# An expert's row capacity cut from 128 to 96 in the mixture stage of a two-layer decoder trunk

## The chip, the cores and the metric

The kernel runs on one core of a Trainium2 chip. The metric is the device time of one execution in microseconds (us); a comparison takes medians over several executions. The instruction streams belong to TensorE (PE; its weight loads are listed apart as PEld), VectorE (DVE), ScalarE (ACT), GpSimd (POOL) and SyncE (SP), which issues most of the DMAs.

## What is computed

Two decoder layers over 256 tokens of width 1024, in float32. Layer 0 is latent attention and retention, then a dense gated feed-forward part; layer 1 is sliding-window and stick-breaking attention, then a mixture of 8 experts of which every token takes 2. The change lies in the mixture:

```python
def _moe(h, router, w_gate, w_up, w_down):
    xf = h.reshape(T, D)
    logits = (xf @ router).astype(jnp.float32)
    top_logits, top_idx = lax.top_k(logits, TOP_K)
    gates = jax.nn.softmax(top_logits, axis=-1)
...
    def expert_block(args):
        xb, e = args
        return (jax.nn.silu(xb @ w_gate[e]) * (xb @ w_up[e])) @ w_down[e]
```

`w_gate` and `w_up` are 1024 x 3584 and `w_down` is 3584 x 1024 for each expert, float32. The 512 choices (256 tokens, two each) are spread over the experts as the router says; the outputs, scaled by the gates, are added to their tokens' rows. The final norm follows.

## The kernel before

**Precision.** Each float32 operand is split in two fp32r parts, a high one (a rounded copy, made by ScalarE) and a low one (the difference, made by VectorE). `mm3` (line 288) multiplies with three matmuls, lines 290, 291 and 292: high by high, high by low, low by high. The first operand is the stationary one, which an instruction of its own loads (LDWEIGHTS in the profile); the second is the moving one.

**The weight stream.** All weights pass through a ring in SBUF: 14 slots of 1 MB in the mixture. SyncE issues a load when VectorE has split the slot's old content. A slot is two units of 128 x 1024; `hi_unit` (line 295) and `lo_unit` (line 301) split a unit into one of four pairs of buffers `w_hi`, `w_lo`, which TensorE gives back when it has multiplied with it.

**One expert** (`moe_pe`, `moe_act`, `moe_dve`, from line 1769 on). The expert's tokens stand in CAP = 128 places. `xe_hi`, `xe_lo` hold their rows turned, 8 blocks of 128 features by CAP places. In the matmuls the token side is stationary and the weights move, 512 columns at a time: `gate_up` gives a bank of [places, 512] for each of 7 chunks of 512 hidden features, ScalarE applies SiLU and VectorE multiplies into `eh`. `turn` (line 1931) transposes `eh` in four matmuls against the identity into bank 6, [features, 4 x CAP]; ScalarE copies it to `hT_hi` and VectorE takes the difference `hT_lo`. `down` multiplies these with `w_down` and accumulates in banks 4 and 5. In such a transpose the data is stationary and the identity moves. The order on TensorE is written by hand, so that each product's inputs were made one chunk earlier.

**Getting and putting rows.** `prepare_pick` compares the places' numbers (`iota`, from 128 x part + 1 on) with the tokens' positions in the expert. `rows_pe` (line 1723) makes token number and gate of each place with four short matmuls. POOL gathers the next expert's rows from DRAM to `xe_rows` (line 1754), and adds the scaled outputs of the expert to the tokens' rows in DRAM, `h_rows` (line 1759); free places go to spare rows behind the 256 real ones. `turn_rows` (line 1706) transposes the gathered rows, eight matmuls. The first expert's rows are gathered by matmul instead (`gather_pe`, line 1699), and the last expert's outputs are put back by matmul with `pickT`.

**The general path.** Every engine runs the eight experts once (`part` 0), then reads the count of the fullest expert and compares it with CAP:

```python
        def overflow(eng, body, most):

            with eng.If(most > CAP):
                body(eng, 1)
```

Where it is larger, all eight experts are run again for the places from 129 to 256.

Of the kernel before, what the change touches and what calls it, by code (L numbers as in the profile page):

```python
# [37 lines left out]
CAP = 128  # L38
# [18 lines left out]
def moe_items():  # L57
# [9 lines left out]
    ident=128, g_ab=8, eps=8, incl=128, negones=128, ones=128, before=128, strict=128, iota=264, cos_m=64, sin_m=64,  # L67
# [10 lines left out]
def trunk(nc, x, consts, decay_t, ab_w_in, w_uq, w_ukv, ab_w_out, f_gate, f_up, f_down,  # L78
          cd_w_in, cd_w_out, router, m_gate, m_up, m_down, moe_gain, final_gain, out):
    with ExitStack() as ctx:  # L80
# [91 lines left out]
        eh = [place(f"eh{i}", [P, FC], at=ARENA + 2048 * i) for i in range(2)]  # L172
# [4 lines left out]
        y_hi = place("y_hi", [P, D], F32R, at=ARENA + 8192)  # L177
        y_rows = place("y_rows", [P, D], at=ARENA + 8192)
        xe_rows = place("xe_rows", [P, D], at=XT_AT + 12288)
        y_lo = place("y_lo", [P, D], F32R, at=XT_AT + 12288)  # L180
        pick = place("pick", [P, TB, CAP], at=ARENA + 12288)
        tok_gate = place("tok_gate", [P, TB, NE + 1], at=ARENA + 13312)
        row_from = place("row_from", [P, 1], U32, at=ARENA + 13440)
        row_next = place("row_next", [P, 1], U32, at=ARENA + 13472)
        row_to = place("row_to", [P, 1], U32, at=ARENA + 13504)
        gate_next = place("gate_next", [P, 1], at=ARENA + 13536)
        place_gate = place("place_gate", [P, 1], at=ARENA + 13568)
        spare_row = place("spare_row", [P, 1], at=ARENA + 13600)
        h_rows = nc.dram_tensor("h_rows", (256 + CAP, D), F32).ap()
        xn_rows = nc.dram_tensor("xn_rows", (256, D), F32).ap()  # L190
        pickT = place("pickT", [P, TB, P], F32R, at=ARENA + 14336)
# [1492 lines left out]
        def gather_act(act, r, q):  # L1684
            act.wait_ge(gather_banked, 2 * q + (r + 1))
            nc.scalar.activation(xe_hi[:, 4 * r:4 * r + 4, :].rearrange("p k t -> p (k t)"), pb[2 + r],
                                 ACT.Copy).then_inc(gather_hi, 1)

        def gather_dve(dve, r, q):
            dve.wait_ge(gather_hi, 2 * q + (r + 1))  # L1690
            nc.vector.tensor_tensor(xe_lo[:, 4 * r:4 * r + 4, :].rearrange("p k t -> p (k t)"), pb[2 + r],  # L1691
                                    f32(xe_hi[:, 4 * r:4 * r + 4, :].rearrange("p k t -> p (k t)")),
                                    ALU.subtract).then_inc(gathered, 1)

        def gather_pe(pe, r):
            for kk in range(4):
                k = 4 * r + kk
                for tb in range(TB):
                    ins = nc.tensor.matmul(pb[2 + r][:, kk * P:kk * P + P], xn[:, tb, k * P:k * P + P],
                                           pick[:, tb, :], start=tb == 0, stop=tb == 1)  # L1700
# [18 lines left out]
        def rows_pe(pe, q):  # L1719

            pe.wait_ge(pick_done, 2 * q + 2)
            for tb in range(TB):
                ins = nc.tensor.matmul(pb[7][:, 0:NE + 1], pick[:, tb, :], tok_gate[:, tb, :], start=tb == 0,
# [3 lines left out]
        def rows_dve(dve, e, q, part):  # L1727

            dve.wait_ge(rows_banked, q + 1)
            found = pb[7][:, 0:1]  # L1730
            nc.vector.tensor_scalar(spare_row, found, 0.0, const("spare"), ALU.is_equal, ALU.mult).then_inc(spare_done, 1)
            nc.vector.tensor_scalar(row_from, found, -1.0, 0.0, ALU.add, ALU.max)
            nc.vector.tensor_copy(gate_next, pb[7][:, one(e + 1)])
# [35 lines left out]
        def moe_act(act, part):  # L1769
            def silu_(c, q):  # L1770
# [3 lines left out]
                nc.scalar.activation(eh[c % 2], pb[2 * (c % 2)], ACT.Silu).then_inc(e_silu, 1)  # L1774

            def turned(c, q):
# [5 lines left out]
                nc.scalar.activation(hT_hi[c % 2].rearrange("p j t -> p (j t)"), pb[6], ACT.Copy).then_inc(hT_done, 1)  # L1782

            def outputs(q, last):
                act.wait_ge(row_ready, q + 1)
                for n in range(2):
# [5 lines left out]
                    nc.scalar.activation(dst[:, n * 512:n * 512 + 512], pb[4 + n], ACT.Copy,  # L1792
# [38 lines left out]
        def moe_dve(dve, part):  # L1831
            def product(c, q):
                dve.wait_ge(*m_used("u", c, q))
                dve.wait_ge(e_silu, 7 * q + (c + 1))
                nc.vector.tensor_tensor(eh[c % 2], eh[c % 2], pb[2 * (c % 2) + 1], ALU.mult).then_inc(e_prod, 1)

            def rest(c, q):
                dve.wait_ge(hT_done, 7 * q + (c + 1))
                nc.vector.tensor_tensor(hT_lo[c % 2].rearrange("p j t -> p (j t)"), pb[6],  # L1839
# [3 lines left out]
            def outputs_rest(q):  # L1843
                for n in range(2):
                    w = slice(n * 512, n * 512 + 512)
                    dve.wait_ge(y_scaled, 2 * q + (n + 3))
                    nc.vector.scalar_tensor_tensor(out=y_lo[:, w], in0=pb[4 + n], scalar=place_gate,
# [10 lines left out]
            def expert(e, q, last):  # L1858
                for c in range(1, NFC):
# [8 lines left out]
                    if c == 1:  # L1868
                        if last:
                            dve.wait_ge(pgt_banked, part + 1)  # L1870
                            nc.vector.tensor_scalar(pickT.rearrange("p b t -> p (b t)"), pb[7][:, 0:256], 0.0, None,
# [42 lines left out]
        def moe_pe(pe, part):  # L1914
            def gate_up(kind, c, q, units=slice(0, 4)):
                bank = pb[2 * (c % 2) + (kind == "u")]
# [9 lines left out]
            def turn(c, q):  # L1926
# [21 lines left out]
            def down_last(q):  # L1948
                pe.wait_ge(hT_lo_done, 7 * q + (LAST + 1))
                units = m_units(("d", LAST))  # L1950
                for t, nn in ((0, 0), (0, 1), (1, 0), (1, 1), (2, 0), (3, 0), (2, 1), (3, 1)):
# [4 lines left out]
                    ins = mm3(pb[4 + nn], hT_hi[LAST % 2][:, t, :], hT_lo[LAST % 2][:, t, :], w_hi[:, buf, w],  # L1956
# [16 lines left out]
            def expert(q, last):  # L1973
                for c in range(1, NFC):
# [3 lines left out]
                    if c == 1 and last:  # L1978
                        pe.wait_ge(rows_done, q + 1)
                        pe.wait_ge(pick_done, 2 * q + 2)  # L1980
                        for tb in range(TB):
                            ins = nc.tensor.transpose(pb[7][:, tb * P:tb * P + P], pick[:, tb, :], const("ident"))
# [161 lines left out]
        def overflow(eng, body, most):  # L2144

            with eng.If(most > CAP):
                body(eng, 1)
# [176 lines left out]
def shape_tables(np):  # L2324
# [11 lines left out]
    t["iota"] = np.broadcast_to(np.arange(264, dtype=f), (P, 264))  # L2336
# [65 lines left out]
```

## Time and profile before

| | |
|---|---|
| median of 3 runs | 1550.05 us (1549.32 to 1550.11) |
| the profiled execution's own time | 1550.45 us |
| its span, first to last instruction | 1548.7 us |
| mean granted TensorE clock | 0.993 |
| TensorE busy | 1514.1 us, 98% of the span |
| weight loads | 1245.4 us, 80% |
| VectorE busy | 1269.4 us, 82% |
| ScalarE busy | 1105.1 us, 71% |
| POOL busy | 25.9 us, 2% |
| bytes read from HBM | 447.33 MB |

How to read it: the profile is one execution. A row of a group of instructions gives the line of the code, the engine, the operation, what it writes and reads, its shapes and its count, then the busy time and the mean duration, and the idle time of the engine in front of it with what ended that. Matmuls overlap: each lasts longer than the distance from its start to the start of the next, and the end is modelled, so the pace of TensorE is read from starts, or from the chain of waits, whose pieces don't overlap. A shape `128*96` of a matmul or a weight load is rows by columns of the stationary operand, and the `128x512` behind it the moving operand or, for a weight load, what is loaded. The granted clock is 1.00 for 2.4 GHz and 0.50 for 1.2 GHz.

### The profile page before, as it was taken

The page shows a single profiled execution, that of the slowest core. Times are in us where ns is not written, and L with a number is a line of the kernel's source. Part 1 is how long each engine was busy: PE and PEld are TensorE (multiplying, and loading weights), DVE is VectorE, ACT ScalarE, POOL GpSimd, SP SyncE. Part 2 cuts the span into 40 slices and gives each one's busy share as a digit, 9 for nine tenths or more (in the row PEclk, how much of TensorE's full clock was granted, in tenths as well). Part 3 has the DMA queues.
Part 4 walks back from the last instruction along what each step waited for, and adds up shares of the span by engine and source line. Part 5 has one row for each costly group of instructions (what it writes and reads, how often), then busy time and mean ns, then how long its engine had stood idle before and what let it go on. Part 6 is the DMA issues. An engine that isn't in the chain of part 4 may idle for free.

```text
span 1548.7 us, 22163 instructions
## 1 busy us (share of the span) xinstructions
PE 1514.1 (98%) x7290; PEld 1245.4 (80%) x7290; DVE 1269.4 (82%) x1553; ACT 1105.1 (71%) x1380; POOL 25.9 (2%) x21
## 2 busy tenths in 40 slices
PE   7999999999999999999999999999999999999997
PEld 6778788888777678888888888888888888888885
DVE  4577576666667668999999999999999999999997
ACT  5565455555466648888888888788788788878885
POOL 0000000000000000000000000000000000000000
PEclk9999999999999989999999999999999999999999
DMA  8433365455544569999999999999999999999970
GB/s 328 168 131 112 129 226 213 163 205 201 190 164 152 187 232 344 377 375 368 389 372 366 387 382 360 387 389 354 389 387 350 394 387 349 399 383 349 403 277 29
DMA packets 193176, 454.88 MB, mean 294 GB/s; under 512 B 8160, under 2 KB 12128, under 8 KB 192864
## 3 DMA queue, kind: packets, MB, share of 16 engines
q1 hardware_dynamic: 190288, 443.69, 77.6%
q0 software_dynamic: 2832, 10.49, 2.7%
q8 instruction: 30, 0.49, 0.1%
q14 instruction: 26, 0.21, 0.0%
HBM read 447.33 MB, written 6.82 MB: 293 GB/s over the span
## 4 chain that ended last, share of the span: by engine, by line
PE 95%; DVE 4%; ACT 1%; issue 0%; DMA 0%; SPq 0%; DVEq 0%; ACTq 0%
PE bank L290 26%; PE bank L292 25%; PE bank L291 25%; PE bank L1431 7%; PE bank L1433 3%; PE bank L1931 2%; DVE w_lo L303 1%; PE bank L360 1%; PE bank L1271 1%; PE bank L788 1%; PE bank L1262 0%; PE bank L777 0%; DVE xT_both L330 0%; PE bank L1706 0%; DMA h<-x_dram 0%
## 5 line engine op out<-in xcount | busy, mean ns | idle before, releaser
L303 DVE TENSOR_TENSOR w_lo<-ring_low,w_hi 128x1024 fp32r<-128x1024 f32 (+2 forms) x442 | 533.5, 1217 | 100.2 <-ACT w_hi L299 76.5
L299 ACT ACTIVATE w_hi<-ring_low 128x1024 fp32r<-128x1024 f32 (+2 forms) x442 | 466.1, 1056 | 134.0 <-PE bank L292 133.6
L303 DVE TENSOR_TENSOR w_lo<-ring,w_hi 128x1024 fp32r<-128x1024 f32 x336 | 404.4, 1222 | 38.0 <-ACT w_hi L299 15.9
L299 ACT ACTIVATE w_hi<-ring 128x1024 fp32r<-128x1024 f32 x336 | 355.1, 1063 | 81.5 <-PE bank L292 81.4
L290 PE MATMUL bank<-w_hi,xe_hi 128*128 128x512 f32 x896 | 353.8, 395 | 0.4 <-DVE xe_lo L1691 0.4
L292 PE MATMUL bank<-w_hi,xe_lo 128*128 128x512 f32 x896 | 349.7, 390 | 0.0
L291 PE MATMUL bank<-w_lo,xe_hi 128*128 128x512 f32 x896 | 348.9, 389 | 0.0
L292 PEld LDWEIGHTS bank<-w_hi,xe_lo 128*128 128x128 f32 x896 | 168.2, 188 | 35.9
L290 PEld LDWEIGHTS bank<-w_hi,xe_hi 128*128 128x128 f32 x896 | 168.3, 188 | 34.2 <-DVE xe_lo L1691 0.6
L291 PEld LDWEIGHTS bank<-w_lo,xe_hi 128*128 128x128 f32 x896 | 168.4, 188 | 34.0
L290 PE MATMUL bank<-w_hi,hT_hi 128*128 128x512 f32 x448 | 177.5, 396 | 0.0
L292 PE MATMUL bank<-w_hi,hT_lo 128*128 128x512 f32 x448 | 176.0, 393 | 0.0
L291 PE MATMUL bank<-w_lo,hT_hi 128*128 128x512 f32 x448 | 175.7, 392 | 0.0
L1431 PE MATMUL bank<-xT_both,w_hi 128*128 128x512 f32 x448 | 159.0, 399 | 0.0
L1433 PE MATMUL bank<-xT_both,w_lo 128*128 128x256 f32 x448 | 126.3, 282 | 0.0
L1431 PEld LDWEIGHTS bank<-xT_both,w_hi 128*128 128x128 f32 x448 | 84.8, 189 | 20.1
L292 PEld LDWEIGHTS bank<-w_hi,hT_lo 128*128 128x128 f32 x448 | 84.2, 188 | 19.0
L291 PEld LDWEIGHTS bank<-w_lo,hT_hi 128*128 128x128 f32 x448 | 84.4, 188 | 18.2
L290 PEld LDWEIGHTS bank<-w_hi,hT_hi 128*128 128x128 f32 x448 | 84.3, 188 | 18.3 <-DVE hT_lo L1839 0.3
L1416 DVE TENSOR_TENSOR w_lo<-ring_low,w_hi 128x1024 fp32r<-128x1024 f32 x56 | 68.5, 1224 | 34.0 <-ACT w_hi L1408 32.5
L290 PE MATMUL bank<-w_hi,xT_both 128*128 128x512 f32 (+3 forms) x224 | 89.2, 398 | 4.7 <-DVE w_lo L303 3.8
L1433 PEld LDWEIGHTS bank<-xT_both,w_lo 128*128 128x128 f32 x448 | 85.3, 191 | 0.3
(301 smaller groups left out, 1621.7 us busy)
## 6 DMA issues: line engine op xcount, KB each, us to landing
ring<-m_gate_dram SPq DMA_DIRECT2D x72, 1024.0 KB, 5.8
ring_low<-m_down_dram SPq DMA_DIRECT2D x72, 1024.0 KB, 6.2
ring<-m_up_dram SPq DMA_DIRECT2D x56, 1024.0 KB, 6.0
ring_low<-m_up_dram SPq DMA_DIRECT2D x56, 1024.0 KB, 6.5
ring_low<-m_gate_dram SPq DMA_DIRECT2D x40, 1024.0 KB, 5.6
ring<-m_down_dram SPq DMA_DIRECT2D x40, 1024.0 KB, 6.8
ring_low<-f_gate_dram SPq DMA_DIRECT2D x14, 1024.0 KB, 5.1
ring_low<-f_up_dram SPq DMA_DIRECT2D x14, 1024.0 KB, 5.4
```

The lines of the kernel that those rows point to most:

```text
L290: nc.tensor.matmul(out_, a_hi, b_hi, start=first, stop=False, **kw)
L291: nc.tensor.matmul(out_, a_hi, b_lo, start=False, stop=False, **kw)
L292: return nc.tensor.matmul(out_, a_lo, b_hi, start=False, stop=last, **kw)
L299: nc.scalar.activation(w_hi[:, buf, 0:width], src, ACT.Copy).then_inc(hi_ready, 1)
L303: nc.vector.tensor_tensor(w_lo[:, buf, 0:width], src, f32(w_hi[:, buf, 0:width]), ALU.subtract).then_inc(split_ready, 1)
L360: ins = nc.tensor.matmul(pb[bank][half_rows(r), cols], v[r][0 if first else 1], a[r][:, src], start=first, stop=not first, skip_group_chec ...
L788: ins = nc.tensor.matmul(pb[((7, 4), (5, 6))[tb][nh]][:, 0:384], latT[:, k, tb * P:tb * P + P], ring[4 + nh][:, k * 384:k * 384 + 384], st ...
L1271: ins = nc.tensor.transpose(pt_bank(i)[:, b * P:b * P + P], p_sb1[i % 2][:, 1 + b * P:1 + b * P + P], const("ident"))
L1416: nc.vector.tensor_tensor(f_split(w_lo, u), f_block(kind, u), f32(f_split(w_hi, u)), ALU.subtract).then_inc(split_ready, 1)
L1431: nc.tensor.matmul(pb[j], w_hi[:, j, w], xT_both[:, :, k, :], start=k == 0, stop=False, skip_group_check=True)
L1433: ins = nc.tensor.matmul(pb[j][:, 0:256], w_lo[:, j, w], xT_hi[:, k, :], start=False, stop=k == KD - 1, skip_group_check=True)
L1931: ins = nc.tensor.transpose(pb[6][:, j * P:j * P + P], eh[c % 2][:, j * P:j * P + P], const("ident"))
```

## The change

CAP becomes 96. Every tile and every bank slice with a place per partition has 96 partitions instead of 128, every one with a place per column has 96 columns. The general path runs the experts again in two further parts, for the places 97 to 192 and 193 to 288, instead of one; the table `iota` becomes longer for that.

```diff
-CAP = 128
+CAP = 96
+PARTS = 3
...
-        eh = [place(f"eh{i}", [P, FC], at=ARENA + 2048 * i) for i in range(2)]
+        eh = [place(f"eh{i}", [CAP, FC], at=ARENA + 2048 * i) for i in range(2)]
...
-        xe_rows = place("xe_rows", [P, D], at=XT_AT + 12288)
+        xe_rows = place("xe_rows", [CAP, D], at=XT_AT + 12288)
...
-                ins = nc.tensor.transpose(pb[2 + r][:, kk * P:kk * P + P], xe_rows[:, k * P:k * P + P],
-                                          const("ident"))
+                ins = nc.tensor.transpose(pb[2 + r][:, kk * CAP:kk * CAP + CAP], xe_rows[:, k * P:k * P + P],
+                                          const("ident")[0:CAP, 0:CAP])
...
-                nc.scalar.activation(hT_hi[c % 2].rearrange("p j t -> p (j t)"), pb[6], ACT.Copy).then_inc(hT_done, 1)
+                nc.scalar.activation(hT_hi[c % 2].rearrange("p j t -> p (j t)"), pb[6][:, 0:4 * CAP], ACT.Copy).then_inc(hT_done, 1)
...
-                bank = pb[2 * (c % 2) + (kind == "u")]
+                bank = pb[2 * (c % 2) + (kind == "u")][0:CAP]
...
-                    ins = nc.tensor.transpose(pb[6][:, j * P:j * P + P], eh[c % 2][:, j * P:j * P + P],
-                                              const("ident"))
+                    ins = nc.tensor.transpose(pb[6][:, j * CAP:j * CAP + CAP], eh[c % 2][:, j * P:j * P + P],
+                                              const("ident")[0:CAP, 0:CAP])
...
-                        ins = mm3(pb[4 + nn], hT_hi[c % 2][:, t, :], hT_lo[c % 2][:, t, :], w_hi[:, buf, w],
+                        ins = mm3(pb[4 + nn][0:CAP], hT_hi[c % 2][:, t, :], hT_lo[c % 2][:, t, :], w_hi[:, buf, w],
...
-                body(eng, 1)
+                for part in range(1, PARTS):
+                    body(eng, part)
```

`xe_hi`, `xe_lo`, `hT_hi`, `hT_lo` and `pick` were written with CAP before and change with it. The engines' lists up to the branch keep their order; shapes change, and what is skipped behind the branch grows. TensorE in the loop over experts, at the transposes of the first chunk, before (here the shape behind a product is the written bank's partitions by the moving columns, behind a transpose the written partitions by columns):

```order
L292 MATMUL bank<-w_hi,xe_lo 128x512
L1927 REGISTER_ALU
L1931 MATMUL bank<-cst,eh_124 128x128 x4
L1918 REGISTER_ALU
L290 MATMUL bank<-w_hi,xe_hi 128x512
L291 MATMUL bank<-w_lo,xe_hi 128x512
```

and now (lines are one higher):

```order
L293 MATMUL bank<-w_hi,xe_lo 96x512
L1928 REGISTER_ALU
L1932 MATMUL bank<-cst,eh_124 128x96 x4
L1919 REGISTER_ALU
L291 MATMUL bank<-w_hi,xe_hi 96x512
L292 MATMUL bank<-w_lo,xe_hi 96x512
```

The products are as many and move as many columns; the transposes write and move 96 columns instead of 128. POOL at the end of part 0 and behind the branch, before:

```order
L1651 TENSOR_LOAD cnt_i
L1651 ISA x2
L1765 DMA h<-h_rows 128x2x1024
L2146 COMPARE_AND_BRANCH
L1745 DMA h_rows<-h 128x2x1024
L1754 DMA xe_rows<-xn_rows,row_from 128x1024
L1759 DMA h_rows<-y_rows,row_to 384x1024
```

and now:

```order
L1652 TENSOR_LOAD cnt_i
L1652 ISA x2
L1766 DMA h<-h_rows 128x2x1024
L2147 COMPARE_AND_BRANCH
L1746 DMA h_rows<-h 128x2x1024
L1755 DMA xe_rows<-xn_rows,row_from 96x1024
L1760 DMA h_rows<-y_rows,row_to 352x1024

```

The indirect transfers have 96 rows instead of 128, and behind the one branch stand two further parts instead of one (the second is not shown).

## Rows read from the trace of the kernel before

**Rows 1.** The page: span, and granted clock in 40 slices of 38.7 us
```profile
span 1548.7 us, 22163 instructions
...
PEclk9999999999999989999999999999999999999999
```

**Rows 2.** Waits, 620 us to the end: who waited for whom, total us, times, longest
```profile
POOL h_rows L1759 <- issue: 419.4, 7, 59.9
...
ACT w_hi L299 <- PE bank L292: 168.2, 564, 0.6
DVE w_lo L303 <- ACT w_hi L299: 19.7, 58, 1.3
...
PE bank L1969 <- DVE y_lo L1847: 0.3, 1, 0.3
```

**Rows 3.** Waits of the SyncE queue, 620 us to the end
```profile
SPq L1636 <- DVE w_lo L303: 696.5, 307, 3.5
```

**Rows 4.** Chain of waits, pieces of three stretches: start us, us, what
```profile
28.71 3.43 PE bank L777 x8
...
46.54 3.87 PE bank L788 x12
...
1052.03 0.87 PE bank L1706 x8
...
1091.76 0.44 PE bank L1931 x4
1092.19 0.35 PE bank L1723 x4
...
1171.63 0.87 PE bank L1706 x8
```

**Rows 5.** Groups of instructions on PE, by form: count, busy us, mean ns, idle before
```profile
L290 PE MATMUL bank<-w_hi,xe_hi 128*128 128x512 f32 x896 | 353.8, 395 | 0.4 <-DVE xe_lo L1691 0.4
...
L290 PE MATMUL bank<-w_hi,hT_hi 128*128 128x512 f32 x448 | 177.5, 396 | 0.0
...
L1931 PE MATMUL bank<-cst,eh 128*128 128x128 f32 x224 | 33.5, 272 | 0.0
...
L1706 PE MATMUL bank<-cst,xe_rows 128*128 128x128 f32 x56 | 7.2, 272 | 0.0
```

**Rows 6.** Timeline of the stage from 900 us: start us, us, engine, line, operation
```profile
900.01 0.39 PE L290 MATMUL bank<-w_hi,xe_hi 128*128 128x512 f32 x1
...
903.18 0.39 PE L292 MATMUL bank<-w_hi,xe_lo 128*128 128x512 f32 x1
```

**Rows 7.** Groups of weight loads (PEld), by form
```profile
L290 PEld LDWEIGHTS bank<-w_hi,xe_hi 128*128 128x128 f32 x896 | 168.3, 188 | 34.2 <-DVE xe_lo L1691 0.6
...
L1931 PEld LDWEIGHTS bank<-cst,eh 128*128 128x128 f32 x224 | 27.7, 140 | 7.3
...
L797 PEld LDWEIGHTS bank<-cst,kcat 128*96 128x96 f32 x16 | 1.8, 125 | 0.3
```

**Rows 8.** Timeline of PE in layer 0, products of 288 columns
```profile
14.24 0.44 PE L291 MATMUL bank<-w_lo,xT_both 128*128 128x288 f32 x1
...
16.64 0.44 PE L292 MATMUL bank<-w_hi,xT_both 128*128 128x288 f32 x1
...
17.47 0.29 PE L290 MATMUL bank<-w_hi,xT_both 128*128 128x288 f32 x1
...
19.33 0.30 PE L292 MATMUL bank<-w_hi,xT_both 128*128 128x288 f32 x1
```

**Rows 9.** Stretches: us, busy (count) by engine, PEclk, DMA share, GB/s
```profile
13.00:17.00 4.00, 3.16 (x13) 3.16 (x14) 2.79 (x5) 3.98 (x8) 0.00 (x0) 0.61 0.96 405
18.00:20.00 2.00, 2.00 (x18) 2.00 (x16) 1.09 (x3) 1.64 (x2) 0.00 (x0) 1.00 1.04 394
...
820.00:920.00 100.00, 100.00 (x452) 82.50 (x451) 92.68 (x91) 81.28 (x84) 3.31 (x2) 1.00 1.03 381
```

**Rows 10.** Groups of instructions on DVE by form, 620 to 1500 us
```profile
L1839 DVE TENSOR_TENSOR hT_lo<-bank,hT_hi 128x512 fp32r<-128x512 f32 x51 | 34.8, 683 | 0.0
```

More of the change, by code:

```diff
@@ L1685, in gather_act @@
             act.wait_ge(gather_banked, 2 * q + (r + 1))
-            nc.scalar.activation(xe_hi[:, 4 * r:4 * r + 4, :].rearrange("p k t -> p (k t)"), pb[2 + r],
+            nc.scalar.activation(xe_hi[:, 4 * r:4 * r + 4, :].rearrange("p k t -> p (k t)"), pb[2 + r][:, 0:4 * CAP],
                                  ACT.Copy).then_inc(gather_hi, 1)
@@ L1690, in gather_dve @@
             dve.wait_ge(gather_hi, 2 * q + (r + 1))
-            nc.vector.tensor_tensor(xe_lo[:, 4 * r:4 * r + 4, :].rearrange("p k t -> p (k t)"), pb[2 + r],
+            nc.vector.tensor_tensor(xe_lo[:, 4 * r:4 * r + 4, :].rearrange("p k t -> p (k t)"), pb[2 + r][:, 0:4 * CAP],
                                     f32(xe_hi[:, 4 * r:4 * r + 4, :].rearrange("p k t -> p (k t)")),
@@ L1722, in rows_pe @@
             for tb in range(TB):
-                ins = nc.tensor.matmul(pb[7][:, 0:NE + 1], pick[:, tb, :], tok_gate[:, tb, :], start=tb == 0,
+                ins = nc.tensor.matmul(pb[7][0:CAP, 0:NE + 1], pick[:, tb, :], tok_gate[:, tb, :], start=tb == 0,
                                        stop=tb == 1)
@@ L1729, in rows_dve @@
             dve.wait_ge(rows_banked, q + 1)
-            found = pb[7][:, 0:1]
-            nc.vector.tensor_scalar(spare_row, found, 0.0, const("spare"), ALU.is_equal, ALU.mult).then_inc(spare_done, 1)
+            found = pb[7][0:CAP, 0:1]
+            nc.vector.tensor_scalar(spare_row, found, 0.0, const("spare")[0:CAP], ALU.is_equal, ALU.mult).then_inc(spare_done, 1)
             nc.vector.tensor_scalar(row_from, found, -1.0, 0.0, ALU.add, ALU.max)
-            nc.vector.tensor_copy(gate_next, pb[7][:, one(e + 1)])
+            nc.vector.tensor_copy(gate_next, pb[7][0:CAP, one(e + 1)])
             dve.wait_ge(spare_done, q + 1)
@@ L1773, in silu_ @@
                 act.wait_ge(h_banked, 7 * q + max(c, 1))
-                nc.scalar.activation(eh[c % 2], pb[2 * (c % 2)], ACT.Silu).then_inc(e_silu, 1)
+                nc.scalar.activation(eh[c % 2], pb[2 * (c % 2)][0:CAP], ACT.Silu).then_inc(e_silu, 1)
             def turned(c, q):
@@ L1834, in product @@
                 dve.wait_ge(e_silu, 7 * q + (c + 1))
-                nc.vector.tensor_tensor(eh[c % 2], eh[c % 2], pb[2 * (c % 2) + 1], ALU.mult).then_inc(e_prod, 1)
+                nc.vector.tensor_tensor(eh[c % 2], eh[c % 2], pb[2 * (c % 2) + 1][0:CAP], ALU.mult).then_inc(e_prod, 1)
             def rest(c, q):
                 dve.wait_ge(hT_done, 7 * q + (c + 1))
-                nc.vector.tensor_tensor(hT_lo[c % 2].rearrange("p j t -> p (j t)"), pb[6],
+                nc.vector.tensor_tensor(hT_lo[c % 2].rearrange("p j t -> p (j t)"), pb[6][:, 0:4 * CAP],
                                         f32(hT_hi[c % 2].rearrange("p j t -> p (j t)")),
@@ L1955, in down_last @@
                         pe.wait_ge(split_ready, UPE * q + (U_MOE + n + 1))
-                    ins = mm3(pb[4 + nn], hT_hi[LAST % 2][:, t, :], hT_lo[LAST % 2][:, t, :], w_hi[:, buf, w],
+                    ins = mm3(pb[4 + nn][0:CAP], hT_hi[LAST % 2][:, t, :], hT_lo[LAST % 2][:, t, :], w_hi[:, buf, w],
                               w_lo[:, buf, w], False, t == 3)
@@ L1981, in expert @@
                         for tb in range(TB):
-                            ins = nc.tensor.transpose(pb[7][:, tb * P:tb * P + P], pick[:, tb, :], const("ident"))
+                            ins = nc.tensor.transpose(pb[7][0:CAP, tb * P:tb * P + P], pick[:, tb, :], const("ident"))
                         ins.then_inc(pgt_banked, 1)
```

32 lines of the change are left out of this document (16 added, 16 removed).

## The prediction

> **What bounds the kernel now.** The page comes first: the core spans 1548.7 us, and from the sixteenth of 40 slices on TensorE has the full clock throughout [rows 1]. That TensorE is also the one that everybody waits for has to be seen elsewhere, in the list of waits from 620 us to the end [rows 2]: ScalarE waited 168.2 us for matmuls in 564 waits, and VectorE 19.7 us for ScalarE, while TensorE waited 0.3 us once, for the last scatter. TensorE is never short of work there. The SyncE queue waited 696.5 us for VectorE to let go of a ring slot [rows 3], so the weight stream is not what is late either. The changed stage is therefore counted on TensorE alone, and everything else only has to stay below it.
>
> The length of one expert is read from the chain: the turning of gathered rows begins at 1052.03 us and again at 1171.63 us [rows 4], so an expert takes 119.60 us. In the stage there are 896 x 3 products with `xe` and 448 x 3 with `hT` [rows 5], 4032 in all, 504 per expert, each with 512 moving columns. Beside them stand 224 transposes of `eh` in 56 groups of four and 56 transposes of gathered rows in 7 groups of eight. A group of four takes 0.44 us and a group of eight 0.87 us on the chain [rows 4], 109 ns each. So an expert spends 36 x 0.109 = 3.9 us on transposes, 0.35 us on the four short matmuls of the row table [rows 4], and 119.60 - 4.3 = 115.3 us on 504 products, 229 ns each. In a quiet stretch products start every 226.4 ns: 14 intervals from 900.01 to 903.18 us [rows 6].
>
> **The products.** CAP is the number of *stationary* columns of a product; the moving operand is the weight, 512 columns before and after. 512 columns at 2.4 GHz are 213.3 ns, so 226.4 ns leaves 13.1 ns that is not streaming. The question on which 4032 products hang is what a stationary operand of 96 columns does to these two numbers. Streaming stays. The load of the stationary operand lies beside the product ahead of it: its record is 188 ns long, within 226 ns, and should become shorter. Its dependence on columns can be read from transposes: 140 ns with 128 stationary columns and, at line 797, 125 ns with 96 [rows 7]. A load that is hidden and becomes shorter gives nothing.
>
> What are the 13.1 ns? No row of before has an fp32r product with fewer than 128 stationary columns, so they are bounded. From below, the plain fp32 matmuls of lines 777 and 788 swap the stationary operand too, and 8 of 512 columns take 3.43 us, 428.8 ns each against 2 x 213.3 of streaming: 2.1 ns over [rows 4]. If 96 columns brought the fp32r product there, each would gain 11.0 ns, 4032 x 11.0 = 44.4 us. From above, a narrow load could come to stand in the open: at (140 - 125) / 32 = 0.47 ns per column, 96 columns are 45 ns in place of 13.1, so 4032 x 31.9 = 128.6 us lost. Between these ends I take zero, because of the nearest rows: fp32r products with 288 columns in layer 0. At full clock they start every 132.9 ns (14 intervals, 17.47 to 19.33 us), 120 ns of streaming and 12.9 over, the same remainder as with 512. Just before, at a granted clock of 0.5 inside a window whose mean is 0.61, they start every 240 ns (10 intervals, 14.24 to 16.64 us) [rows 8, 9], and 288 columns at 1.2 GHz are 240 ns: the remainder is gone. A part of the load that stood in the open would double at half the clock, to 26 ns, and it doesn't. So the remainder looks like a fixed step of starting a product, which knows nothing of its columns.
>
> The Trainium skill speaks against this reading: "TensorE: Matmul & The Clock Gate", section on weight-path perf modes, says that fast weight load is on where there are 128 weights and the type is not FP32, and gives 128/4 = 32 cycles for it in theory. 32 cycles at 2.4 GHz are 13.3 ns, which is what the rows leave over; with 96 columns the fast load would then be off. By that rule the sum would be one of the two ends above. The half-clock rows speak against it, and so does the load record of an fp32r product, which at 188 ns is longer than that of a transpose and not shorter.
>
> **The transposes.** Their moving operand is the identity, now 96 columns instead of 128, and this is what does change on TensorE. The fp32 rows give two passes per column: 12 matmuls of 384 columns take 3.87 us, 322.5 ns each, and 8 of 512 take 428.8 [rows 4], which is 0.83 ns per column and 2.1 to 3 ns fixed. That line gives 109 ns at 128 columns, just what the transposes take, and 82.5 at 96. So 26.7 ns each: 224 x 26.7 = 6.0 us and 56 x 26.7 = 1.5 us, all on the path, since there is no idle time on TensorE in front of them or behind. The bounds are this and zero. Zero holds if the load sets their pace: the matmuls with 9 moving columns don't go below 0.35 / 4 = 88 ns in the mean [rows 4]. But their load record is as long as the products', the transposes' one is 48 ns shorter [rows 7]; I take the full gain.
>
> **What else changes.** The copies and differences of 4 x CAP columns (`xe_hi`, `xe_lo`, `hT_hi`, `hT_lo`) lose a quarter of their columns; 683 ns of `hT_lo` [rows 10] lose at most 171. They lie beside products. VectorE is 92.7 us busy in 100 [rows 9], 110.9 us of an expert of 119.6, and after the change below 110 of 118.6: it remains covered. Only before the first product TensorE waits for the first `xe_lo`: a quarter of one copy and one difference is at most 0.3 us, taken as 0.2. SiLU, the gate product and the scaled rows have 96 partitions instead of 128 and the same 512 columns per partition, so they cost what they did. The first gather, 16 fp32 matmuls, counts nothing; its 5.66 us less a quarter, 1.4 us, is its end. Each indirect transfer moves 96 rows instead of 128; POOL has 419.4 us of idle time before the scatters [rows 2], so this is covered; were they late, TensorE would wait at line 1997. The two further parts are skipped by the one branch that skipped one part: the reference's router gives the eight experts 49, 66, 46, 70, 69, 61, 86 and 65 places of the 512, the fullest below 96.
>
> **The sum** is 6.0 + 1.5 + 0.2 = 7.7 us. The profiled execution took 1550.45 us, so 1542.75; the median of the runs shown lies 0.40 lower, at 1550.05, which gives 1542.4 us, 0.5% faster.
>
> **The rivals.**
> *Nothing to be measured:* the transposes keep their pace, bound by their load, and the products too. For it: the 9-column matmuls show that a load can set a pace. Against: the shorter load of a transpose. 1550.05 - 0.2 = 1549.9 us. Chance 0.17.
> *The remainder goes with the columns:* three quarters of 13.1 ns, 3.3 x 4032 = 13.2 us more, 1529.2 us. For it: nothing but that both are per stationary operand; against: the half clock. 0.10.
> *The remainder goes altogether*, as in fp32: 44.4 us more, 1498.0 us. VectorE would then have 110 us of work in an expert of some 113, and the gain might be cut. 0.05.
> *Slower:* the load of 96 columns no longer hides behind the product ahead, at lines 290 to 292, and 45 ns stand in the open in place of 13.1. From +1.9 ns per product on, the gain is eaten (7.7 / 4032); at 31.9 ns it is 1542.4 + 128.6 = 1671.0 us. For it: every fp32r product of before is of full width, so nothing shows that a narrow one is handled alike. Against: a load of 188 ns has 38 ns to spare within a product of 226, and a shorter one has more. It is also one outcome of the skill's rule above, with the case before it as the other. 0.12.
> *The change doesn't do what it says:* an expert above 96 would run both further parts, 16 x 119.6 us more, 3456 us. The counts exclude it but for ties and rounding: 0.01.
>
> **The numbers.** The forecast itself gets 0.55. With "nothing" and "with the columns" it makes 0.82, so the range goes from 1528 to 1552 us, the ends of these two with a few tenths to two microseconds for the runs themselves. Within 0.2%, 3.1 us, is what a measurement of this kernel can't tell from no change. Faster: 0.55 + 0.10 + 0.05 = 0.70; same: 0.17; slower: 0.12 + 0.01 = 0.13.
>
> **What would show it.** In the profile of the changed kernel the chain should have groups of four transposes at 0.33 us and of eight at 0.66; the distance between two groups of eight should be 118.6 us; products should start every 226 ns in quiet stretches, with load records of some 160 ns. If products start at 223 or at 216 ns, one of the two faster rivals holds; at 230 or more, the slower one. If the list of waits shows TensorE waiting for VectorE's `w_lo`, the cover of VectorE was thinner than read here. The prediction is wrong if the start distance of the products moves by more than 1 ns, since 4032 of them make 4 us of it.

## The result and the profile after

The changed kernel takes 1551.95 us in the median (1550.68 to 1553.05, 20 runs), the kernel before 1549.92 us on the same chip (1549.06 to 1550.96, 20 runs). The ratio is 1.0015, with a 95% interval from 1.0008 to 1.0021: 0.15% slower, where 0.5% faster was forecast. That lies within the 0.2% named as what a measurement can't tell from no change, though the interval doesn't reach 1. The time is 0.05 us short of the range's upper end. Between forecast and measurement are 9.6 us, and these have to be found.

The page of the changed kernel (its own time was 1552.63 us), to be read against [rows 1]:

```profile
span 1550.7 us, 22163 instructions
...
PE 1516.7 (98%) x7290; PEld 1132.4 (73%) x7290; DVE 1260.0 (81%) x1553; ACT 1096.9 (71%) x1380; POOL 24.8 (2%) x21
...
PEclk9999999999999989999999999999999999999999
```

The clock is as before, so it explains nothing. The span is 2.0 us longer and TensorE is 2.6 us busier, although it moves fewer columns in 280 transposes.

The chain of waits of the changed kernel, the same places as in [rows 4] (start us, us, what):

```profile
1052.37 0.66 PE bank L1707 x8
...
1092.27 0.33 PE bank L1932 x4
1092.60 0.27 PE bank L1724 x4
...
1172.35 0.66 PE bank L1707 x8
```

A group of eight takes 0.66 us where it took 0.87, a group of four 0.33 for 0.44. The row table's matmuls take 0.27 for 0.35, which had not been counted. Per expert that is 36 x 0.082 + 0.27 = 3.24 us in place of 4.30, 1.06 less. But the distance of the two groups of eight is 119.98 us, where it was 119.60. So 504 products take 116.74 us instead of 115.30: 231.6 ns each in place of 228.8. 2.8 ns x 4032 are 11.5 us lost, against 8 x 1.06 = 8.5 us won; the stage from its first product to its last grew by 3.0 us (579.23 to 1535.52 us before, 578.10 to 1537.41 after). The changed kernel reached the stage 1.1 us earlier in its profiled execution. Ahead of it nothing but addresses and the small first gather had changed; what part of the 1.1 us is theirs comes below.

The pace can be seen directly. (Times in the lines are rounded to 0.01 us, so a pace over 23 intervals is good to 0.4 ns and one over 14 to 0.7.) The timeline of PE in the changed kernel, the stretch of [rows 6]:

```profile
899.99 0.40 PE L291 MATMUL bank<-w_hi,xe_hi 128*96 128x512 f32 x1
900.23 0.39 PE L292 MATMUL bank<-w_lo,xe_hi 128*96 128x512 f32 x1
900.46 0.39 PE L293 MATMUL bank<-w_hi,xe_lo 128*96 128x512 f32 x1
...
903.23 0.39 PE L293 MATMUL bank<-w_hi,xe_lo 128*96 128x512 f32 x1
```

14 intervals take 3.24 us, 231.4 ns each; before it was 226.4 in an even beat. What did not change is the reading that TensorE sets the pace. The list of waits, 620 us to the end, as in [rows 2]:

```profile
POOL h_rows L1760 <- issue: 419.1, 7, 59.9
...
ACT w_hi L300 <- PE bank L293: 177.6, 557, 0.6
DVE w_lo L304 <- ACT w_hi L300: 62.7, 324, 1.3
...
PE bank L1970 <- DVE y_lo L1848: 0.3, 1, 0.3
```

TensorE still waits 0.3 us in the whole stage. VectorE's waits for ScalarE's `w_hi` rose from 19.7 to 62.7 us and ScalarE's for TensorE from 168.2 to 177.6: both got shorter work and a slower TensorE, and wait for it. The stretch 820 to 920 us, for [rows 9], and VectorE's `hT_lo`, for [rows 10]:

```profile
820.00:920.00 100.00, 100.00 (x450) 70.15 (x449) 91.80 (x90) 79.96 (x83) 3.15 (x2) 1.00 1.02 377
```

```profile
L1840 DVE TENSOR_TENSOR hT_lo<-bank,hT_hi 128x384 fp32r<-128x384 f32 x51 | 28.1, 550 | 0.0
```

VectorE is busy 91.8 us in 100 and TensorE all 100; `hT_lo` lost 133 ns. The cover of VectorE held. The load records, for [rows 7]:

```profile
L291 PEld LDWEIGHTS bank<-w_hi,xe_hi 128*96 128x96 f32 x896 | 144.6, 161 | 58.7
...
L1932 PEld LDWEIGHTS bank<-cst,eh 96*128 96x128 f32 x224 | 24.9, 140 | 9.1
```

The product's load is 161 ns, as forecast, 27 ns shorter than before, and the products are slower nonetheless.

**What the trace of before already had.** Four of seven chunks of an expert (0, 2, 4, 6) take `hT` from ARENA + 4096, the three others from XT_AT + 4096. The timeline of PE in the kernel before, first and last product of an even chunk's `down`:

```profile
909.35 0.40 PE L290 MATMUL bank<-w_hi,hT_hi 128*128 128x512 f32 x1
...
914.70 0.40 PE L292 MATMUL bank<-w_hi,hT_lo 128*128 128x512 f32 x1
```

That is 5.35 us for 23 intervals, 232.6 ns each, against 226.4 for `xe` [rows 6]. The odd chunks' `hT` runs at 226.7 ns, away from transposes, as `xe` does. The same instruction form, the same 128 columns, on the same engine with nothing to wait for ran 6 ns slower with another tile. In the changed kernel the same stretch reads:

```profile
909.36 0.39 PE L291 MATMUL bank<-w_hi,hT_hi 128*96 128x512 f32 x1
...
914.66 0.39 PE L293 MATMUL bank<-w_hi,hT_lo 128*96 128x512 f32 x1
```

5.30 us, 230.4 ns. So one pace got worse and the other better.

### The profile page after: what moved, and what is told of

The parts are those of the page before. It is cut to its first block, busy times and chain, and to the rows that moved or that the text cites. A ratio compares the mean times of both kernels' runs of the same rounds, so it can differ in the third digit from the quotient of the medians.

```text
span 1550.7 us, 22163 instructions
## 1 busy us (share of the span) xinstructions
PE 1516.7 (98%) x7290; PEld 1132.4 (73%) x7290; DVE 1260.0 (81%) x1553; ACT 1096.9 (71%) x1380; POOL 24.8 (2%) x21
## 4 chain that ended last, share of the span: by engine, by line
PE 95%; DVE 3%; ACT 1%; issue 1%; DMA 0%; SPq 0%; DVEq 0%; ACTq 0%
PE bank L291 26%; PE bank L293 26%; PE bank L292 26%; PE bank L1432 7%; PE bank L1434 3%; PE bank L1932 1%; PE bank L361 1%; DVE w_lo L304 1%; PE bank L1272 1%; PE bank L789 0%; PE bank L1263 0%; PE bank L778 0%; DVE xT_both L331 0%; PE bank L1700 0%; DMA h<-x_dram 0%
## 5 line engine op out<-in xcount | busy, mean ns | idle before, releaser
L291 PE MATMUL bank<-w_hi,xe_hi 128*96 128x512 f32 x896 | 355.4, 397 | 0.0
L293 PE MATMUL bank<-w_hi,xe_lo 128*96 128x512 f32 x896 | 354.0, 395 | 0.0
L292 PE MATMUL bank<-w_lo,xe_hi 128*96 128x512 f32 x896 | 351.6, 392 | 0.0
L293 PEld LDWEIGHTS bank<-w_hi,xe_lo 128*96 128x96 f32 x896 | 144.3, 161 | 62.9
L292 PEld LDWEIGHTS bank<-w_lo,xe_hi 128*96 128x96 f32 x896 | 144.9, 162 | 60.5
L291 PEld LDWEIGHTS bank<-w_hi,xe_hi 128*96 128x96 f32 x896 | 144.6, 161 | 58.7
L291 PE MATMUL bank<-w_hi,hT_hi 128*96 128x512 f32 x448 | 177.0, 395 | 0.0
L293 PE MATMUL bank<-w_hi,hT_lo 128*96 128x512 f32 x448 | 176.0, 393 | 0.0
L292 PE MATMUL bank<-w_lo,hT_hi 128*96 128x512 f32 x448 | 175.6, 392 | 0.0
L292 PEld LDWEIGHTS bank<-w_lo,hT_hi 128*96 128x96 f32 x448 | 72.4, 162 | 30.4
```

The lines of the kernel that those rows point to most:

```text
L291: nc.tensor.matmul(out_, a_hi, b_hi, start=first, stop=False, **kw)
L292: nc.tensor.matmul(out_, a_hi, b_lo, start=False, stop=False, **kw)
L293: return nc.tensor.matmul(out_, a_lo, b_hi, start=False, stop=last, **kw)
```

## Theories

**Width.** A product with 96 stationary columns has a slower pace than one with 128, wherever the operand stands.
**Address.** The pace depends on where the stationary operand begins. Worked out from the placements of the program, XT_AT is a multiple of 256 bytes and ARENA stands 128 bytes behind one. The change moves it: `iota` grows from 264 to 296 columns, 128 bytes, and all tiles placed behind the constants move by as much, which puts ARENA on a multiple. At the same time blocks of 96 columns are 384 bytes apart instead of 512, so every other block of `xe` and `hT` begins 128 bytes behind a multiple.
**The load in the open**, the mechanism of the prediction's slower rival, was the third.

## The experiments

All ratios are to the kernel before on the same chip; a bracket is the 95% interval. "Period" is the distance of two groups of eight transposes on the chain, 119.60 us before and 119.98 after; "pace" is the distance between starts of products.

### The address alone

The kernel before with nothing changed but the length of `iota` (label e2_shift128):

```diff
-    ... iota=264, ...
+    ... iota=296, ...
-    t["iota"] = np.broadcast_to(np.arange(264, dtype=f), (P, 264))
+    t["iota"] = np.broadcast_to(np.arange(296, dtype=f), (P, 296))
```

> The kernel before with the table of place numbers 32 columns longer and nothing else, so all tiles behind the constants (hT of the even chunks, fT of the dense layer) lie 128 bytes higher. Address theory: the down products of the even chunks go from 232.9 to 226.7 ns, 768 x 6.2 = 4.8 us, and fT, 336 products, from 232 to 227, 1.7 us: about 1543 us. Width theory: nothing moves, 1549.9 us.

Measured: 1544.66 us against 1549.70, ratio 0.9965 [0.9951, 0.9979], 5.0 us faster by 32 columns that nobody reads. Its chain and the timeline of an even chunk's `down`:

```profile
1048.63 0.87 PE bank L1706 x8
...
1167.56 0.87 PE bank L1706 x8
```

```profile
906.80 0.39 PE L290 MATMUL bank<-w_hi,hT_hi 128*128 128x512 f32 x1
...
912.02 0.39 PE L292 MATMUL bank<-w_hi,hT_lo 128*128 128x512 f32 x1
```

The period fell from 119.60 to 118.93 us, and the 23 intervals from 5.35 to 5.22 us, 227.0 ns each: the even chunks now run as `xe` does. The odd chunks, whose `hT` did not move, kept their 226.7. Of a product's operands in the even chunks only the stationary one moved (the weights' buffers and the banks stayed), so its place is what counts there, and the change contained a gain of about 5 us that the forecast didn't see.

Two more lengths ask whether it is a matter of 256 bytes. With 280 columns (e5_shift64) the even `hT` starts 192 bytes behind a multiple, with 360 (e6_shift384) on a multiple of 256 that is none of 512.

```diff
-    ... iota=264, ...
+    ... iota=280, ...
```

> The kernel before with everything behind the constants 64 bytes higher, so hT of the even chunks and fT begin 192 bytes behind a multiple of 256 instead of 128. Address theory with a granule of 256 bytes: still off it, so 232.9 ns as before or near it and 1549.7 us. If 128 bytes were the granule and 128 off one of the good cases in it, now worse than before, above 1551 us.

Measured: 1545.53 us against 1549.50, ratio 0.9972 [0.9962, 0.9983]. Its even chunk:

```profile
907.45 0.39 PE L290 MATMUL bank<-w_hi,hT_hi 128*128 128x512 f32 x1
...
912.72 0.39 PE L292 MATMUL bank<-w_hi,hT_lo 128*128 128x512 f32 x1
```

5.27 us, 229.1 ns: between 227.0 and 232.6. The expectation of 232.9 was missed: a pace that only asked "on a multiple or not" would have stayed at 232.6. The offset acts in degrees.

```diff
-    ... iota=264, ...
+    ... iota=360, ...
```

> The kernel before with everything behind the constants 384 bytes higher: hT of the even chunks and fT begin on an odd multiple of 256 bytes instead of 128 behind one (in e2_shift128 it was a multiple of 512). If a multiple of 256 is enough: 226.7 ns for all down products and 1544.7 us, as e2_shift128. If it needs 512 there: about 1549 us; the tiles of xe lie on an odd multiple of 256 already and run at 226.7 ns, which speaks for the first.

Measured: 1543.35 us against 1550.17, ratio 0.9960 [0.9946, 0.9973], with the same even beat of 226.5 ns in that chunk (905.55 to 910.76 us, 23 intervals). So a multiple of 256 bytes is enough. The dense feed-forward's `fT`, also stationary and behind ARENA, does the same: its products start every 232.6 ns at 128 bytes behind a multiple, 229.0 at 192 and 227.1 on one.

### The transposes alone

The kernel before, with both kinds of transposes writing and moving 96 columns and products as before (e4_transposes). It leaves places 97 to 128 out of the turning; no expert fills them.

```diff
-    ins = nc.tensor.transpose(pb[6][:, j * P:j * P + P], eh[c % 2][:, j * P:j * P + P],
-                              const("ident"))
+    ins = nc.tensor.transpose(pb[6][:, j * P:j * P + 96], eh[c % 2][0:96, j * P:j * P + P],
+                              const("ident")[0:96, 0:96])
...
```

> The kernel before with only the transposes of eh and of the gathered rows moving 96 columns (places 97 to 128 are not turned; no expert fills them). Address and width theory alike: products as before, 280 transposes x 26.7 ns = 7.5 us less, 1542.4 us. A third theory, that the shorter transposes put the products out of a regular beat: 1550 to 1552 us with products at 231 ns.

Measured: 1543.69 us against 1549.70, ratio 0.9959 [0.9946, 0.9973], 6.0 us faster where this part had been given 7.5.

```profile
1049.23 0.66 PE bank L1706 x8
...
1168.11 0.66 PE bank L1706 x8
```

The period is 118.88 us, 0.72 less, not the 36 x 0.027 = 0.97 by which the transposes became shorter. Where the rest stays is seen at a group of four, in the timeline of this kernel and, below, of the one before (`x4` is the group):

```profile
867.98 0.49 PE L1931 MATMUL bank<-cst,eh 96*128 96x96 f32 x4
868.26 0.47 PE L290 MATMUL bank<-w_hi,xe_hi 128*128 128x512 f32 x1
868.57 0.39 PE L291 MATMUL bank<-w_lo,xe_hi 128*128 128x512 f32 x1
868.80 0.40 PE L292 MATMUL bank<-w_hi,xe_lo 128*128 128x512 f32 x1
```

```profile
869.62 0.60 PE L1931 MATMUL bank<-cst,eh 128*128 128x128 f32 x4
869.97 0.48 PE L290 MATMUL bank<-w_hi,xe_hi 128*128 128x512 f32 x1
870.29 0.40 PE L291 MATMUL bank<-w_lo,xe_hi 128*128 128x512 f32 x1
870.52 0.40 PE L292 MATMUL bank<-w_hi,xe_lo 128*128 128x512 f32 x1
```

From the start of the group to the third product behind it passes 0.82 us, and 0.90 before: 0.08 us of the 0.11. The products behind a group start 0.31 or 0.32 and 0.23 us apart in both kernels, so their unevenness is not new. The missing quarter is lost already at the first product, which starts 0.28 us behind the group's start in place of 0.35: the fourth transpose's part of the gain does not reach it. Over all 56 groups the median distance to the third product fell from 904 to 817 ns.

### The width alone

The kernel before, with products that load and write 96 columns from unmoved tiles (e3_narrow); transposes stay at 128. Places 97 to 128 are left out of the products.

```diff
-    bank = pb[2 * (c % 2) + (kind == "u")]
+    bank = pb[2 * (c % 2) + (kind == "u")][0:96]
...
-    ins = mm3(bank, xe_hi[:, k, :], xe_lo[:, k, :], ...
+    ins = mm3(bank, xe_hi[:, k, 0:96], xe_lo[:, k, 0:96], ...
...
-    ins = mm3(pb[4 + nn], hT_hi[c % 2][:, t, :], hT_lo[c % 2][:, t, :], ...
+    ins = mm3(pb[4 + nn][0:96], hT_hi[c % 2][:, t, 0:96], hT_lo[c % 2][:, t, 0:96], ...
```

> The kernel before with only the products of the experts narrowed to 96 stationary columns of the blocks that stay 128 wide (places 97 to 128 are left out of the products; no expert fills them). Address theory: load records of 161 ns, but the pace per item as before, 1549.9 us. Width theory: products at 231.5 ns, 4032 x 2.9 = 11.7 us more, 1561.6 us.

Measured: 1556.12 us against 1549.70, ratio 1.0039 [1.0025, 1.0053], 6.4 us slower. Neither theory had this by itself. `xe` products, on a multiple of 256 bytes as before, now start every 230.0 ns (17 intervals, 900.04 to 903.95 us), 3.6 ns more: that is width. (Here and below width means the stationary columns together with the written partitions of the bank, which are the same number here and were not varied apart.) Those of an even chunk:

```profile
911.52 0.39 PE L290 MATMUL bank<-w_hi,hT_hi 128*96 128x512 f32 x1
911.75 0.40 PE L291 MATMUL bank<-w_lo,hT_hi 128*96 128x512 f32 x1
911.99 0.39 PE L292 MATMUL bank<-w_hi,hT_lo 128*96 128x512 f32 x1
...
916.85 0.39 PE L292 MATMUL bank<-w_hi,hT_lo 128*96 128x512 f32 x1
```

5.33 us, 231.7 ns, where 128 columns had 232.6: off the multiple, width costs nothing further. The two effects are real and do not add up: the start costs 6 ns with 128 columns and 1.7 with 96. That is one reason why the kernel lost 6.4 us and not 4032 x 3.6 ns. The other is that the first twelve distances behind transposes did not rise, 237.6 ns in the mean before and 237.1 here. Over all products of the stage the mean distance rose from 230.0 to 231.7 ns.

### Both, one after the other

The changed kernel with blocks of 128 columns in the four tiles, of which 96 are used, so that every block begins on a multiple of 256 bytes (e1_padded); ScalarE and VectorE write the 96 used columns of each block:

```diff
-        xe_hi = place("xe_hi", [P, KD, CAP], F32R, at=XT_AT)
+        xe_hi = place("xe_hi", [P, KD, P], F32R, at=XT_AT)
...
-        hT_hi = [place(f"hT_hi{i}", [P, 4, CAP], F32R, ...
+        hT_hi = [place(f"hT_hi{i}", [P, 4, P], F32R, ...
...
-                        ins = mm3(bank, xe_hi[:, k, :], xe_lo[:, k, :], ...
+                        ins = mm3(bank, xe_hi[:, k, 0:CAP], xe_lo[:, k, 0:CAP], ...
```

> The changed kernel with the 96 columns of each block of xe and hT kept 512 bytes apart instead of 384; same work, still 96 stationary columns. Address theory (a product is slow where its stationary block does not begin on a multiple of 256 bytes): all 4032 products at 226.7 to 227.5 ns, transposes as short as in the changed kernel, so about 1536 us. Width theory (a load of 96 columns itself makes the pace of 231.5 ns): 1552 us, as the changed kernel.

Measured: 1545.90 us against 1549.70, ratio 0.9977 [0.9967, 0.9987], between the 1536 and 1552 us of the two theories. The products of `xe`:

```profile
899.16 0.39 PE L291 MATMUL bank<-w_hi,xe_hi 128*96 128x512 f32 x1
...
902.61 0.39 PE L291 MATMUL bank<-w_hi,xe_hi 128*96 128x512 f32 x1
```

15 intervals in 3.45 us are 230.0 ns, and an even chunk's are 230.0 too. The distance of the blocks explains a part, 231.5 to 230.0 ns, and not the whole: 226.7 does not come back. That the distance acts through the blocks' starts is likely, not shown. In favour: with blocks 512 bytes apart in e3_narrow, a start 128 bytes behind a multiple already gave 96 columns 231.7 ns; and in the changed kernel's quiet stretches the distances behind products of `xe` blocks that begin on a multiple are 231.2 ns in the mean, behind those that begin off one 232.3.

The same kernel, and now the products also load 128 columns; the last 32 hold what stood there before, and the output rows that come of them are read by nobody (e7_wide). Transposes, transfers and the loop's logic keep 96; the copies and differences that make `xe` and `hT` go over 512 columns again, as before the change.

```diff
-                bank = pb[2 * (c % 2) + (kind == "u")][0:CAP]
+                bank = pb[2 * (c % 2) + (kind == "u")]
...
-                        ins = mm3(pb[4 + nn][0:CAP], hT_hi[c % 2][:, t, :], ...
+                        ins = mm3(pb[4 + nn], hT_hi[c % 2][:, t, :], ...
...
-                    ins = nc.tensor.transpose(pb[6][:, j * CAP:j * CAP + CAP], ...
+                    ins = nc.tensor.transpose(pb[6][:, j * P:j * P + CAP], ...
```

> The changed kernel with 96 places, but with products over 128 stationary columns in blocks 512 bytes apart (columns 97 to 128 of a block hold whatever the bank held and give rows that nobody reads); transposes move 96 columns, hT lies 128 bytes higher than before. Both findings so far (128 columns make 226.7 ns, 96 make 230.0; a block beginning off a multiple of 256 bytes costs more): products as in e2_shift128, mean 227.2 ns, transposes as in e4, so 1544.7 - 6 to 7.5 = 1537 to 1539 us, below both kernels. If the two gains don't add: 1543 to 1545 us.

Measured: **1536.61 us** against 1549.50, ratio 0.9915 [0.9901, 0.9928], a little below the 1537 to 1539 expected where both gains add. It beats both kernels, the one before by 12.9 us and the changed one, over their ratios, by some 15.

```profile
1045.20 0.66 PE bank L1707 x8
...
1163.31 0.66 PE bank L1707 x8
```

```profile
904.37 0.39 PE L291 MATMUL bank<-w_hi,hT_hi 128*128 128x512 f32 x1
...
909.58 0.39 PE L293 MATMUL bank<-w_hi,hT_lo 128*128 128x512 f32 x1
```

The period is 118.11 us, and the 23 intervals of an even chunk take 5.21 us, 226.5 ns. Transposes are at 0.66 us, as in the changed kernel. Going back from here to the change, with each kernel's distance to its own runs of before: 32 columns fewer in the products cost 9.1 us (-12.9 to -3.8), blocks 384 bytes apart 5.8 us more (-3.8 to +2.0). Each of the first two distances is good to about 2 us. The stages of the profiled executions agree: 944.5, 953.8 and 959.3 us, steps of 9.3 and 5.5.

### Other widths

Is it 96, or anything below 128? Three kernels on the base of e2_shift128, where all tiles begin on a multiple of 256 bytes and blocks are 512 bytes apart, with products of 112, 64 and 120 columns. The edit is that of e2_shift128 and that of e3_narrow with 112, 64 or 120 for 96. The first and the last leave free places alone out; that with 64 leaves places 65 to 96 out, which some experts fill, so it leaves out work that the reference asks for. Its instructions are as many, and of the same length in moving columns.

> e2_shift128 (all stationary blocks on multiples of 256 bytes) with the expert products narrowed to 112 stationary columns (places above 112 are left out; no expert fills them). Step theory (any width below 128 has the pace of 96): pattern 228 to 232, mean 230.0 ns, 1544.7 + 4032 x 2.8 ns = 1556 us. Gradual theory (the pace follows the columns): about 228.4 to 228.7 ns, 1550 us.

> As e8 with 64 stationary columns (places 65 to 96 are left out of the products, so the rows of fuller experts lack their part). Step theory: 230.0 ns and 1556 us as with 112 and 96. Gradual theory: 227.2 + 2 x 2.8 = 232.8 ns, 1567 us.

> As e8 with 120 stationary columns. If every width below 128 loses the even beat of 226.7 ns: a repeating pattern of other intervals with a mean between 229 and 233 ns, 1551 to 1556 us. If only much narrower loads lose it: 226.7 ns and 1544.7 us as in e2_shift128.

Measured, with 96 from e1_padded and 128 from e2_shift128 beside them (medians 1553.93 us with 64, 1555.57 with 112, against 1549.50; 1566.53 with 120, against 1550.17, over 10 us above the most that was expected). The mean pace is over the start distances between products of the stage, without the first one behind a group of transposes or the row table (3902 distances each):

| columns | ratio to before | period, us | load record, ns | mean pace, ns |
|---|---|---|---|---|
| 64 | 1.0028 [1.0017, 1.0038] | 120.32 | 134 | 230.1 |
| 96 | 0.9977, transposes shorter as well | 119.29 | 161 | 230.0 |
| 112 | 1.0040 [1.0026, 1.0054] | 120.28 | 174 | 230.05 |
| 120 | 1.0107 [1.0092, 1.0123] | 121.91 | 181 | 233.3 |
| 128 | 0.9965 [0.9951, 0.9979] | 118.93 | 188 | 227.2 |

Groups of weight loads (PEld) by form, of the kernels with 64, 112 and 120 columns:

```profile
L290 PEld LDWEIGHTS bank<-w_hi,xe_hi 128*64 128x64 f32 x896 | 120.3, 134 | 81.8
```

```profile
L290 PEld LDWEIGHTS bank<-w_hi,xe_hi 128*112 128x112 f32 x896 | 156.1, 174 | 47.6
```

```profile
L290 PEld LDWEIGHTS bank<-w_hi,xe_hi 128*120 128x120 f32 x896 | 162.5, 181 | 43.9
```

The loads lie on one line with 161 and 188: 54 ns for 64 columns, 0.84 ns for each. A load in the open would make 64 columns the fastest and each further column dearer. The mean pace is equal at 64, 96 and 112, worst at 120 and best at 128. Two stretches, 64 columns and 120:

```profile
894.57 0.39 PE L290 MATMUL bank<-w_hi,hT_hi 128*64 128x512 f32 x1
...
903.54 0.40 PE L290 MATMUL bank<-w_hi,xe_hi 128*64 128x512 f32 x1
```

```profile
896.30 0.39 PE L290 MATMUL bank<-w_hi,hT_hi 128*120 128x512 f32 x1
...
901.89 0.40 PE L290 MATMUL bank<-w_hi,xe_hi 128*120 128x512 f32 x1
```

39 intervals in 8.97 us are 230.0 ns, 24 in 5.59 us are 232.9. Neither a gradual effect of columns nor a plain step between 128 and the rest was right: 128 is best, but the others differ among themselves. With 112 the mean of 230.05 hides two paces: of 58 stretches of products between transposes, 47 settle at about 228.9 ns and 10 at 233.3, and a stretch keeps its pace to its end. One of the slower ones, 24 intervals in 5.60 us:

```profile
839.77 0.39 PE L290 MATMUL bank<-w_hi,xe_hi 128*112 128x512 f32 x1
...
845.37 0.39 PE L290 MATMUL bank<-w_hi,hT_hi 128*112 128x512 f32 x1
```

So its equality with 64 and 96 is one of means alone. The third theory, the load in the open, is refuted: the record of a load of 64 columns, 134 ns, has 96 ns to spare within its product of 230, and the product is 3 ns slower than that of 128. The longest load of all has the best pace.

The Trainium skill's rule, weighed in the prediction from "TensorE: Matmul & The Clock Gate", section on weight-path perf modes, makes 128 columns a case of their own. The pace agrees that they are; the load records do not show a fast load, since 188 ns at 128 continues the line through 181, 174, 161 and 134. The Trainium skill gives those 32 cycles for fp8, in the same table, and the operands here are fp32r; that they come to the 13.3 ns left over is then no support for the rule. Neither of the two ends that the rule led to came: not 11.0 ns won per product and not 31.9 lost, but 2.8 lost (227.2 to 230.0).

## Why the prediction was wrong

**The step that failed** is, in its words, "Between these ends I take zero", with the reason that the remainder "looks like a fixed step of starting a product, which knows nothing of its columns". It does know them. At full clock it is 13.3 ns in the even beat only, and that beat was seen with 128 columns on a multiple of 256 bytes; with fewer columns or another start the remainder is about 16 to 20 ns. The half-clock rows [rows 8, 9] were read rightly, and the widths agree with them that no part of the load stands in the open. They did not say that the remainder has no other source, and 288 moving columns with 128 stationary ones say nothing of 96. The zero had been taken from rows at one width, and it carried 4032 products. With every block on a multiple, the width cost 9.1 us (e7_wide to e1_padded; the mean of all start distances in the stage rose from 228.7 to 231.0 ns). The 11.5 us that the products lost between the two kernels are a net: +9.1 for the width, +5.8 for the distance of blocks, -5.3 for the shift, and about 2 us of the transposes' gain that is lost again at the products behind them.

**What was not costed** is the placement. The change made the iota table longer and the blocks shorter; the prediction gives neither a price. The first was worth 5.0 us for the change (e2_shift128), the second 5.8 us against it (e1_padded to the change). That the place of a tile matters could be read from the trace of before: its mean of 229 ns against 226.4 in the quiet stretch was put down to nothing, and the slow half of it was `hT` of the even chunks at 232.6.

**Right in kind, off in size:** the transposes. Each fell to 82 ns as forecast, groups to 0.33 and 0.66 us, but the term of 7.5 us measured 6.0, since a quarter of a group's gain does not reach the products behind it; "all on the path" was too much. The row table's 0.08 us per expert was missing: its matmuls of 9 moving columns fell from 88 to 68 ns each with 96 stationary columns, so 88 ns was no lower bound. The 0.2 us before the first product came to about 0.1: from the first gather's start to that product 6.06 us passed before and 5.95 after.

**Right:** TensorE alone sets the stage; VectorE's cover holds; load records are 161 ns, where some 160 were forecast; POOL's transfers stay covered (419.1 us of idle time before the scatters in place of 419.4); and there is no second pass over the experts.

**The rivals.** "Nothing to be measured" has the nearest time, 1549.9, and the wrong reasons, for transposes did become faster. Its time came near by luck, since two gains (transposes, shift) met two losses (width, distance). The two faster ones are refuted. The slower one had the right sign, and it named the point that decides: from +1.9 ns per product on the gain is eaten, and the net was +2.8 (228.8 to 231.6). Its mechanism, the load in the open, and its price of 31.9 ns were wrong. Likewise it is luck that the time lies inside the range: neither of the two theories that span it is what happened.

**Adding up.** On the stage: the shift of addresses -5.3 us and the shorter transposes -5.6 (e2_shift128 and e4_transposes, 956.3 to 951.0 and 950.7), the row table 7 x 0.08 = -0.6; together -11.5, and e7_wide, which has these three, took 11.8 us less. That the gains add is a test that could have failed. The steps from there, +9.1 and +5.8 on the whole kernel, were taken as differences up to the changed kernel's +2.0, so their sum tests nothing; the test is the stages' 9.3 and 5.5 us. Ahead of the stage the 336 products of the dense feed-forward part with `fT` went from 232.6 to 227.1 ns with the shift, 1.8 us, and its products of line 1431 gave back about 0.8 (the next section), which together is near the 1.1 us seen. That agreement is weak: in e1_padded, with the same code and addresses ahead of the stage, the stage began at 581.22 us in place of 578.10.

## What stays open

What in the chip makes the beat uneven is not shown; width and start are shown as conditions, not as a mechanism. The starts in the narrow kernels follow patterns of three to six products with steps of 224 to 236 ns, the same in each expert, and after a group of transposes even the full-width products need several before their beat returns. Why 120 columns are the worst isn't explained either. And the start of the stationary operand is not all that a shift does: the dense feed-forward's products of line 1431 (1432 in the changed kernel) have `w_hi` stationary and `xT_both` moving, which both lie where they did, and yet the distance behind them rose from 233.5 to 235.3 ns (448 products, without those over 300 ns) with the very shift that made others faster. Products of 128 columns on blocks 384 bytes apart weren't tried.

## What to carry to other kernels

In a stream of fp32r products like this one, where each loads its own stationary operand and moves 512 columns, try the stationary operand 128 columns wide and on a multiple of 256 bytes, even where fewer columns are needed; the columns saved in the transposes are worth having by themselves. A longer table of constants moves every tile placed behind it, so compare the pace tile by tile, from start distances, before and after an edit that seems to touch no tile. And a remainder that was read at one width is known at that width alone.

## What the hardware showed that was not expected

- The start address of a stationary fp32r operand changes the pace: 226.5 to 227.0 ns on a multiple of 256 bytes, 229.1 at 192 bytes behind one, 232.6 at 128, for the same products of 512 columns with 128 stationary ones. With 96 stationary columns it is 230.0 on a multiple and 231.7 at 128 behind one.
- Fewer stationary columns make a product slower: about 230 ns in the mean at 64, 96 and 112, 233.3 at 120, 227.2 at 128, while its load record falls by 0.84 ns per column.
- 32 unread columns in a table made the kernel 5.0 us faster.
- With 112 stationary columns a stretch of products settles at one of two paces, 228.9 or 233.3 ns, and keeps it until the next transposes.
